# The first microseconds of a five-layer network: inputs in halves, panels ahead of constants, square sums among the first panels

## The reference, cut to what matters

```
def first_block(x, norm_mix_g, ...):
    for i in range(DEPTH):
        h = rmsnorm(x, norm_mix_g[i])
        if i % 3 == 0:
            y = short_conv_mixer(h, a_w_in[ia], a_conv_w[ia], a_w_out[ia])
        ...
        x = x + y
        x = x + swiglu(rmsnorm(x, norm_ffn_g[i]), f_w13[i], f_w2[i])

def rmsnorm(x, g):
    return x * lax.rsqrt(jnp.mean(x * x, axis=-1, keepdims=True) + 1e-6) * g

def short_conv_mixer(h, w_in, conv_w, w_out):
    b_gate, c_gate, u = jnp.split(h @ w_in, 3, axis=-1)
    return (b_gate * depthwise_conv3(c_gate * u, conv_w)) @ w_out
```

## Time and profile before

| what | value |
|---|---|
| time, median of three runs | 1812.35 us (1811.17 to 1813.92) |
| the profiled execution's own time | 1806.41 us |
| its span in the profile | 1804.6 us |
| PE busy | 1741.7 us, 97% of the span |
| DVE busy | 1231.5 us, 68% |
| ACT busy | 983.6 us, 55% |
| bytes moved | 290.12 MB |

### The profile page before, as it was taken

How to read it: one execution, slowest core, us unless ns; L and a number is a source line. 1 busy time by engine, 2 the same in 40 slices (tenths; PEclk the granted TensorE clock), 3 DMA queues, 4 the chain that set the end, 5 groups by cost and what they waited for, 6 DMA issues and landing times.

```text
span 1804.6 us, 37578 instructions
## 1 busy us (share of the span) xinstructions
PE 1741.7 (97%) x13784; PEld 1647.0 (91%) x13784; DVE 1231.5 (68%) x2017; ACT 983.6 (55%) x1368; POOL 12.8 (1%) x20
## 2 busy tenths in 40 slices
PE   7999999999999988999999999999999999999997
PEld 7999999898999987569999999999999777799997
DVE  6886665487766578788666678766566656576654
ACT  4467744365775445226774446775454644467742
POOL 0000200000000000000000000000000000000000
PEclk9999999999999999999999999999999999999999
DMA  6556564433656564204566455656454332255561
GB/s 207 172 196 231 188 211 146 131 107 105 198 186 207 166 195 137 82 1 153 187 185 222 130 176 183 198 186 230 164 173 154 125 132 70 71 173 188 184 215 67
DMA packets 79399, 290.12 MB, mean 161 GB/s; under 512 B 9723, under 2 KB 12124, under 8 KB 79196
## 3 DMA queue, kind: packets, MB, share of 16 engines
q1 hardware_dynamic: 79324, 289.12, 49.9%
HBM read 288.03 MB, written 1.05 MB: 160 GB/s over the span
## 4 chain that ended last, share of the span: by engine, by line
PE 86%; DVE 9%; issue 2%; ACT 2%; DMA 1%; DVEq 0%; SPq 0%; ACTq 0%
PE bank L490 24%; PE bank L492 24%; PE bank L491 24%; DVE wlo L1418 3%; PE bank L780 2%; PE bank L759 1%; PE bank L699 1%; DVE conv_cv L1526 1%; DVE rinv L1424 1%; PE bank L843 1%; PE bank L941 1%; PE bank L678 1%; PE bank L951 0%; DMA raw<-in_w 0%; PE bank L914 0%
## 5 line engine op out<-in xcount | busy, mean ns | idle before, releaser
L490 PE MATMUL bank<-xh,whi 128*128 128x256 f32 (+1 forms) x2736 | 776.0, 284 | 11.7 <-DVE wlo L1418 11.3
L491 PE MATMUL bank<-xl,whi 128*128 128x256 f32 (+1 forms) x2736 | 772.9, 282 | 0.0
L492 PE MATMUL bank<-xh,wlo 128*128 128x256 f32 (+1 forms) x2736 | 772.0, 282 | 0.0
L1038 ACT CAST whi<-raw 128x1024 fp32r<-128x1024 f32 (+1 forms) x490 | 538.0, 1099 | 366.4 <-PE bank L492 319.4
L1418 DVE TENSOR_TENSOR wlo<-raw,whi 128x1024 fp32r<-128x1024 f32 (+1 forms) x491 | 629.5, 1282 | 4.8 <-ACT whi L1038 2.7
L490 PEld LDWEIGHTS bank<-xh,whi 128*128 128x128 f32 x2736 | 519.2, 190 | 27.2 <-issue 15.7
L492 PEld LDWEIGHTS bank<-xh,wlo 128*128 128x128 f32 x2736 | 520.0, 190 | 0.0
L491 PEld LDWEIGHTS bank<-xl,whi 128*128 128x128 f32 x2736 | 516.5, 189 | 0.1
L490 PE MATMUL bank<-ffn_hh,whi 128*128 128x256 f32 x880 | 246.7, 280 | 0.0
L492 PE MATMUL bank<-ffn_hh,wlo 128*128 128x256 f32 x880 | 246.7, 280 | 0.0
L491 PE MATMUL bank<-ffn_hl,whi 128*128 128x256 f32 x880 | 245.7, 279 | 0.0
(11 more groups left out here) (317 smaller groups left out, 2033.3 us busy)
## 6 DMA issues: line engine op xcount, KB each, us to landing
raw<-in_w SPq DMA_DIRECT2D x414, 512.0 KB, 3.6
raw<-in_w SPq DMA_DIRECT2D x80, 704.0 KB, 4.1
att_bias<-in_bias SPq DMA_DIRECT2D x4, 512.0 KB, 5.8
hy_w<-in_filt_w SPq DMA_DIRECT2D x8, 256.0 KB, 4.5
hy_decay<-in_decay SPq DMA_DIRECT2D x4, 512.0 KB, 5.3
mla_uq<-in_uq SPq DMA_DIRECT2D x1, 1152.0 KB, 5.0
x<-in_xT SPq DMA_DIRECT2D x1, 1024.0 KB, 5.9
out<-x SPq DMA_DIRECT2D x8, 128.0 KB, 2.0
```

What stands on the lines that cost most here:

```text
L490: pe.matmul(ps, whi[:, slot, wc], hi[:, k, cols], start=first, stop=False)
L491: pe.matmul(ps, whi[:, slot, wc], lo[:, k, cols], start=False, stop=False)
L492: mm = pe.matmul(ps, wlo[:, slot, wc], hi[:, k, cols], start=False, stop=last)
L1038: nc.scalar.copy(whi[:, p % RING, 0:k * P], raw[:, p % RING, 0:k * P]).then_inc(panel_hi, 1)
```

## The change

SP loads x in two halves of four slices with `vec` between them. Panels 0 and 1 follow, then `con`, panels 2 and 3, the filter's inputs, and the META columns of x last. The one semaphore for four loads becomes four. ACT casts panels 0 and 1 before it squares x. DVE starts when the first half of x and `vec` are there; it splits panel 0 behind slice 1, panel 1 behind slice 3 and panel 2 behind slice 7. PE has no work ahead of the first panels: the filter's product comes behind panel 3, and the eight matmuls with ones are spread over the slices 4 to 7 of the first two panels, two behind each slice.

```diff
@@ SyncE
-        sp.dma_start(x[:, :, A], a["xT"]).then_inc(start_loaded, 16)
-        sp.dma_start(x[:, :, 0:META], a["metaT"]).then_inc(start_loaded, 16)
-        sp.dma_start(vec[:], a["vec"]).then_inc(start_loaded, 16)
-        sp.dma_start(con[:], a["con"]).then_inc(start_loaded, 16)
-        sp.dma_start(filt_in[:], a["filt_in"]).then_inc(filt_loaded, 16)
-        sp.dma_start(filt_w2[:], a["filt_w2"]).then_inc(filt_loaded, 16)
+        sp.dma_start(x[:, 0:C // 2, A], a["xT"][:, 0:C // 2]).then_inc(x_loaded, 16)
+        sp.dma_start(vec[:], a["vec"]).then_inc(x_loaded, 16)
+        sp.dma_start(x[:, C // 2:C, A], a["xT"][:, C // 2:C]).then_inc(x_rest, 16)
...
-                panels(ph, 0, 4)
+                panels(ph, 0, 2)
+                sp.dma_start(con[:], a["con"]).then_inc(con_loaded, 16)
+                panels(ph, 2, 2)
+                sp.dma_start(filt_in[:], a["filt_in"]).then_inc(filt_loaded, 16)
+                sp.dma_start(filt_w2[:], a["filt_w2"]).then_inc(filt_loaded, 16)
+                sp.dma_start(x[:, :, 0:META], a["metaT"]).then_inc(start_loaded, 16)
                 panels(ph, 4, 20)
@@ TensorE, end of first_panels
+                if k >= 4 and not norm:
+                    first_total(2 * k - 8, norm_cols)
+
+        def first_total(k0, cols):
+
+            if k0 == 0:
+                pe.wait_ge(con_loaded, 16)
+                pe.wait_ge(first_squares, 1)
+            for k in (k0, k0 + 1):
+                mm = pe.matmul(bank[7][:, cols], ones, cm["cv"][:, k, :], start=k == 0, stop=k == C - 1)
+            if k0 + 2 == C:
+                mm.then_inc(norm_total, 1)
@@ TensorE, product: behind panels 2 and 3 of in0
+                if norm == 0:
+                    filter_layer(0)
@@ TensorE, start
-        pe.wait_ge(start_loaded, 64)
-        filter_layer(0)
-        total(0, A)
@@ ScalarE
-        act.wait_ge(start_loaded, 64)
-        nc.scalar.activation(cm["cv"][:], x[:, :, A], ACT.Square).then_inc(first_squares, 1)
...
             nc.scalar.copy(whi[:, p, 0:K8 * P], raw[:, p, 0:K8 * P]).then_inc(panel_hi, 1)
+            if p == 1:
+                act.wait_ge(x_loaded, 32)
+                act.wait_ge(x_rest, 16)
+                nc.scalar.activation(cm["cv"][:], x[:, :, A], ACT.Square).then_inc(first_squares, 1)
+        act.wait_ge(start_loaded, 16)
@@ GpSimd
-        pool.wait_ge(start_loaded, 64)
+        pool.wait_ge(con_loaded, 16)
@@ VectorE
-        dve.wait_ge(start_loaded, 64)
         for m in range(C):
+            if m % (C // 2) == 0:
+                dve.wait_ge(x_rest if m else x_loaded, 16 if m else 32)
...
-            if m in (3, 5, 7):
-                p = m // 2 - 1
+            if m in (1, 3, 7):
+                p = (1, 3, 7).index(m)
...
+        dve.wait_ge(start_loaded, 16)
+        dve.wait_ge(con_loaded, 16)
         norm = 0
```

More of the change, by code:

```diff
@@ L300, in build @@
     start_loaded = sem("start_loaded")
+    x_loaded, x_rest, con_loaded = sem("x_loaded"), sem("x_rest"), sem("con_loaded")
     filt_loaded = sem("filt_loaded")
@@ L513, in first_panels @@
                         mm.then_inc(panel_used, 1)
-        def total(norm, cols):
[L517 to L525, removed]
+                if k >= 4 and not norm:
[8 more added lines that the diff above has]
+                mm.then_inc(norm_total, 1)
+        def total(norm, cols):
+            pe.wait_ge(sum_added, SUMS * norm)
+            pe.matmul(bank[7][:, cols], ones, sumsq[:, cols], start=True, stop=True).then_inc(norm_total, 1)
         def product(name, hi, lo, cols, ready, norm=None):
```

## The result

| | before | changed |
|---|---|---|
| median of seven runs each, us | 1812.19 (1806.52 to 1813.92) | 1819.63 (1817.6 to 1825.03) |
| the profiled execution's own time, us | 1806.41 | 1819.28 |
| its span, us | 1804.6 | 1817.5 |

The ratio of the changed kernel to the one before is 1.0053 (95% interval 1.0039 to 1.0068): 0.5% slower, 9.6 us (7.1 to 12.3). The two medians lie only 7.4 us apart and the two profiled executions 12.9 us, both in their spans and in their times; the experiments show where this spread comes from.

A forecast was written before the change was run, and what follows sets the result against it. PE was taken as the limit up to panel 7, whose end everything later hangs on. Terms of 8.2 + 0.7 + 1.6 = 10.5 us on 1812.35 gave 1822.8 us, range 1818.0 to 1825.5.

The forecast's parts named there:

- Panel 0 lands earlier: Loads at the start: panel 0 lands at 8.5 us instead of 9.6, with 274 KB taken from ahead of it.
- From landing to the first matmul: Casts and splits ahead of PE's product: 6.48 us, so PE begins at 15.0 instead of 16.34, -1.4 us.
- The sums among the product: First two panels on PE: eight float32 matmuls with ones at 0.43 us each add 3.5 us.
- The slow first stretch: Start of the product on PE: matmuls run slowly at first, 1.4 to 2.7 us lost, taken as +2.0.
- The late norm: Ahead of panel 3: its first matmul waits for the norm, 33.05 instead of 24.89, +8.2 us with all terms so far.
- The filter's product: Between panels 3 and 4 on PE: the moved product adds 0.7 us that nothing hides.
- The clock after the gap: Behind PE's 4.0 us gap ahead of panel 3: the granted clock falls, +1.6 us likeliest, 0 at the other end.
- From panel 7 on nothing changes: Behind panel 7: order and work are those of before, so the 10.5 us reach the end whole.
- Rival 4: From panel 8 on: the DVE-bound stretch absorbs PE's delay; 1812.4 us, no change; chance 0.07.
- Rival 2: Start: it gains nothing, PE begins at 16.3; 1824.2 us; chance 0.08.
- Rival 3: Ahead of panel 3: no wait for the norm, only moved work counts, 4.8 us, 1817.2 us; chance 0.08.
- Rival 1: Behind the gap ahead of panel 3: the clock stays up; 1821.2 us; chance 0.20.

The follow-up runs named there:

- e1: The changed kernel with ACT's wait for the META columns moved from behind the last cast to ahead of panel 3's cast; ratio to the kernel before 1.0044.
- e2: The changed kernel with all eight matmuls with ones ahead of slice 4 of the first two panels; ratio to the kernel before 1.0030.
- e3: The changed kernel with all eight matmuls with ones ahead of the product again, behind ACT's square; ratio to the kernel before 1.0008.
- e6: The changed kernel with 28 float32 passes, whose result nothing uses, on PE ahead of the product; ratio to the kernel before 1.0058.
- e9: The changed kernel once more, unchanged; panel 7 evicted at 52.13 us, span 1822.2 us.
- e8: The changed kernel: sums ahead of slice 4, META wait ahead of panel 3's cast, cu filled at start, panels 0 and 1 split behind slice 3; ratio 1.0006.
- e7: The changed kernel with the filter's product between panels 2 and 3 instead of behind panel 3; ratio to the kernel before 1.0064.
- e4: The kernel before with PE's part alone: sums in pairs behind slices 4 to 7, filter's product behind panel 3; ratio to the kernel before 1.0058.

## Why the prediction was right, point by point

The direction, the place and the mechanism held: 1819.63 us against 1822.8 forecast, inside the range; +9.6 us by the ratio against +10.5. At the eviction of panel 7, where the sum was made, it is 12.4 to 13.5, so the sum was 2 to 3 us too small there while the end time came out 3 us lower than forecast. That the end time lies so near is partly luck; with 12.4 to 13.5 us in the sum the forecast would have been 1824.8 to 1825.9, at the upper edge of the range. By its steps:

- *Panel 0 lands earlier.* Forecast 8.5, seen 9.00, and from 8.50 to 9.29 in the kernels with the changed loads (e1, e2, e3, e6 to e9). Right in sign; 0.5 us short in the profiled execution.
- *From landing to the first matmul.* Forecast 6.48, seen 15.52 - 9.00 = 6.52. The table load is followed by the cast 0.02 us later, as rows 5 had it. That PE gains little because DVE stands behind ACT was right: 4.00 us of idle time. e8, in which slices 2 and 3 go ahead of that stand (2.77 us are left of it), begins at 13.85.
- *The sums among the product.* 3.5 forecast, and 3.62 busy for the sixteen instructions in e8; in the changed kernel the whole stretch from 15.52 to panel 2 took 11.1 us, forecast 5.7 + 3.5 + 2.0 = 11.2.
- *The slow first stretch.* 2.0 forecast, 2.1 by e6, and 1.8 to 2.7 over the other executions. It lasted from 15.52 to 20.1.
- *The late norm.* The mechanism held, and e2, e3 and e8 show that it holds most of the loss. The term most in error is the hand-over from the last sum to the root, taken as 0.2 us: the root's table load (1.28 us) was not on the path before, and I did not see that the new wait for the META columns puts it there. e1 gives it back. Panel 3 began at 35.02 instead of 33.05, and the gap of PE was 5.24 instead of 4.0.
- *The filter's product.* 0.7 forecast. e7 removes it from PE's path, together with some slow time; for the two, 2.0 us.
- *The clock after the gap.* It fell, as forecast, but for longer: the granted clock is 0.50 from about 33.8 to 40.6, so with the filter's product from panel 3 to the eviction of panel 7 it is 3.4 us more than before, where 0.7 + 1.6 was forecast. This term was 1.1 us too small. In e1, e4 and e7 the slow stretch was half as long, some 3.4 us, and in e1 the same difference is 2.4 us.
- *From panel 7 on nothing changes.* Right within 1 us: the root near 127 us still has 11.9 to 13.1 us of the shift, and some 1 us comes back in all. The forecast compared one execution with the median of other executions; the rest varies by 6 us, about half of the shift at panel 7.
- *The bounds.* The low end was added up wrongly: 10.5 - 1.3 - 0.6 - 1.6 is 7.0, not 6.7. And 0.01 was left for anything faster beside a chance of 0.03 for faster. Neither bears on the result.

Rival 4 (absorbed) is excluded: all kernels still have their shift of panel 7, in part less the 0.5 us above, at the next root 75 us later, and the ratios of the larger shifts (the changed kernel, e1, e2, e4, e6, e7) show it at the end. The 4 to 5 us of e3 and e8 can't be told from nothing there. Rival 2 (the start gains nothing) didn't occur: the product begins at 15.52 and 15.11. Rival 3 (no wait for the norm) is excluded by the gap. Rival 1 (the clock stays up) didn't occur behind gaps of 3.80 to 5.25 us and did behind one of 2.40.

What stays open is why the rest varies. It varies in three stretches alone, and in the two that tell, the longer ones have the lower granted clock. TensorE's slow stretches account for it by size: in the last one, 0.03 of 304.6 us against 0.01 of 297.6 is some 6 of the 7 us, an estimate from rounded figures. Why the clock falls more often in one execution than in another no run tested.

## What to carry to other kernels

Work that stands ahead of a long product while its operands are still being prepared cost nothing here, and it also took the slow first microseconds of TensorE; moved in among the product it cost its full length, and whatever waits for it came late too. That holds as long as the work is ready in time: in e3 the sums stand ahead again, but their squares come behind two casts, and the product begins 4.2 us later than in the kernel before. Before moving a reduction, follow its result: here the sums fed the root, the norm and, through DVE's fixed order, the split of panel 3, and this chain was covered only because it reached DVE at 18.75, 6.1 us ahead of panel 3's first matmul. Look also at what a moved load makes others wait for: the wait for the META columns put a table load on the path. Compare such changes at a landmark that all variants share and that lies ahead of the stretches that vary, since the end of an execution of 1800 us varies by more than most changes of its start are worth.

## What the runs showed of the hardware that was not expected

- A function table load moves with the waits around it. With one wait between the last cast and the root it runs right behind the cast (16.29 in e1); with two it runs behind the later one (27.03 in the changed kernel). That is 1.3 us for a wait that itself cost nothing: in e1 the columns are there when ACT comes to the cast of panel 3, at 15.3.
- Halving a transfer did not use the queue better. From 3.5 to 5.0 us whole x moved at 367 to 391 GB/s in both executions of the kernel before. x in halves with `vec` between them moved at 231 to 251 in the first execution of the changed kernel, at 323 to 332 in the second and at 291 to 354 in e1, e2 and e3, which have the same loads. Panel 0 landed at 9.00, 8.60, 9.29, 8.50 and 8.89, in this order, which doesn't follow the rate in this stretch. Whether the halves or the `vec` between them hold the rate down was not separated.
- At the start of the profile the granted clock doesn't show the slow level: it reads 1.00 from 15.5 to 17.5 us in the changed kernel, where 9 matmuls run in 2 us and 16 in the 2 us from 20 on. The distance of the starts shows it.
- A gap of PE of 2.40 us left the granted clock at 1.00; gaps of 3.80, 3.91, 4.62, 5.24 and twice 5.25 us were all followed by 0.50, for some 3.4 us behind the first three and some 6.8 behind the others.
